# Four of the shift's sixteen conditioning steps moved from slots 49-55 to slots 96-100, the scale's steps one per slot behind them

## The reference

```python
mod = (jax.nn.silu(c) @ w_ada + b_ada)[:, None, :]
sh1, sc1, gt1, sh2, sc2, gt2 = jnp.split(mod, N_MOD, axis=-1)
h = rmsnorm(x, g_pre_mix) * (1.0 + sc1) + sh1
m, ... = token_mixer(h, w_in, ..., w_out, ..., k_past, v_past, s0)
x = x + gt1 * rmsnorm(m, g_post_mix)
h = rmsnorm(x, g_pre_ffn) * (1.0 + sc2) + sh2
f = (silu(h @ w_ffn_gate) * (h @ w_ffn_up)) @ w_ffn_down
x = x + gt2 * rmsnorm(f, g_post_ffn)
```

## Time and profile before

| | us |
|---|---|
| runs | 1507.1, 1503.08, 1507.56; median 1507.1 |
| the profiled execution: its own time | 1503.11 |
| its span, first to last instruction | 1501.4 |
| TensorE busy | 1439.7 (96%) |
| VectorE busy | 913.3 (61%) |
| ScalarE busy | 660.7 (44%) |
| mean granted clock of TensorE | 0.987 |

### The profile page before, as it was taken

One profiled execution on the slowest core, in us unless ns is written; L12 is line 12 of the kernel. 1 busy time (PEld: TensorE's weight loads), 2 busy tenths in 40 slices (PEclk: granted clock), 3 DMA queues, 4 the chain that ended last, 5 costly groups with the idle time before them and its releaser, 6 DMA issues.

```text
span 1501.4 us, 29221 instructions
## 1 busy us (share of the span) xinstructions
PE 1439.7 (96%) x11274; PEld 1274.0 (85%) x11274; DVE 913.3 (61%) x1501; ACT 660.7 (44%) x1277; POOL 105.2 (7%) x205
## 2 busy tenths in 40 slices
PE   7779999998899999998999999999999999999997
PEld 2247787887568787796899999999999999999997
DVE  2243588995687666457657666566665665446444
ACT  1023477776655544336434434444344343334333
POOL 1000311112322200100000000000000000200000
PEclk9979999999899999999999999999999999999999
DMA  9999999999999978996766565665656555855552
GB/s 370 421 362 360 389 387 402 369 333 397 385 373 326 338 259 281 393 328 257 264 184 182 168 193 172 184 179 168 194 177 185 177 171 186 235 182 181 178 179 94
DMA packets 139043, 396.56 MB, mean 264 GB/s; under 512 B 13130, under 2 KB 17393, under 8 KB 126145
## 3 DMA queue, kind: packets, MB, share of 16 engines
q1 hardware_dynamic: 117730, 319.39, 62.9%
q0 software_dynamic: 21232, 76.10, 13.4%
HBM read 382.14 MB, written 11.21 MB: 262 GB/s over the span
## 4 chain that ended last, share of the span: by engine, by line
PE 80%; DMA 12%; DVE 3%; ACT 2%; issue 1%; POOLq 0%; SPq 0%; POOL 0%; DVEq 0%; ACTq 0%
PE ps L1907 23%; PE ps L1908 23%; PE ps L1909 23%; PE ps L1841 4%; DMA ada_s<-in_w_ada 3%; DMA raw<-in_w_in 2%; DMA v_page<-in_cache_v 2%; DMA k_page<-in_cache_k 2%; DMA ada_r<-in_w_ada 2%; PE ps L2039 2%; DMA x_keep<-x_t 1%; PE ps L1965 1%; DVE k_page L1275 1%; DMA k_page<-in_cache_v 1%; PE ps L1884 1%
## 5 line engine op out<-in xcount | busy, mean ns | idle before, releaser
L1907 PE MATMUL ps<-h_hi,w_hi 128*128 128x264 f32 x2304 | 665.7, 289 | 7.6 <-DVE h_lo L1213 3.6
L1908 PE MATMUL ps<-h_lo,w_hi 128*128 128x264 f32 x2304 | 656.5, 285 | 0.0
L1909 PE MATMUL ps<-h_hi,w_lo 128*128 128x264 f32 x2304 | 655.9, 285 | 0.0
L1907 PEld LDWEIGHTS ps<-h_hi,w_hi 128*128 128x128 f32 x2304 | 435.9, 189 | 53.4 <-issue 38.3
L1729 DVE TENSOR_TENSOR w_lo<-raw,w_hi 128x1024 fp32r<-128x1024 f32 x256 | 309.5, 1213 | 275.4 <-ACT w_hi L1018 274.1
L1018 ACT ACTIVATE w_hi<-raw 128x1024 fp32r<-128x1024 f32 x264 | 278.4, 1059 | 405.0 <-PE ps L1909 393.9
L1908 PEld LDWEIGHTS ps<-h_lo,w_hi 128*128 128x128 f32 x2304 | 435.3, 189 | 0.1
L1909 PEld LDWEIGHTS ps<-h_hi,w_lo 128*128 128x128 f32 x2304 | 434.2, 188 | 0.0
L1225 DVE TENSOR_TENSOR w_lo<-raw,w_hi 128x1024 fp32r<-128x1024 f32 x136 | 166.2, 1223 | 162.4 <-ACT w_hi L702 155.1
L702 ACT ACTIVATE w_hi<-raw 128x1024 fp32r<-128x1024 f32 x128 | 134.9, 1055 | 193.4 <-PE ps L1909 162.4
L1908 PE MATMUL ps<-act_lo,w_hi 128*128 (+1 forms) x704 | 200.4, 285 | 0.0
(11 more groups left out here) (336 smaller groups left out, 1211.6 us busy)
## 6 DMA issues: line engine op xcount, KB each, us to landing
ada_r<-in_w_ada SPq DMA_DIRECT2D x64, 1024.0 KB, 9.4
raw<-in_w_in SPq DMA_DIRECT2D x96, 512.0 KB, 8.3
raw<-in_w_ffn_gate SPq DMA_DIRECT2D x88, 512.0 KB, 3.7
raw<-in_w_ffn_up SPq DMA_DIRECT2D x88, 512.0 KB, 3.8
raw<-in_w_ffn_down SPq DMA_DIRECT2D x88, 512.0 KB, 4.1
ada_s<-in_w_ada SPq DMA_DIRECT2D x32, 1024.0 KB, 13.2
k_page<-in_cache_k POOLq DMA_DIRECT2D x64, 512.0 KB, 7.5
v_page<-in_cache_v POOLq DMA_DIRECT2D x38, 512.0 KB, 7.7
```

The lines of the kernel that those rows point to most:

```text
L1907: mm(out, w_hi, xh, start=first, stop=False)
L1908: mm(out, w_hi, xl, start=False, stop=False)
L1909: return mm(out, w_lo, xh, start=False, stop=last)
```

## The change

Part 3 gets 12 steps (n = 16 to 27, slots 25 to 47) and is turned in slot 55 as before. Its last four steps (n = 28 to 31) go to slots 96, 97, 98 and 100, sum up in bank 7 by themselves, are turned in slot 101 and are added on DVE to what `mod_t` holds. Part 4's sixteen steps go to slots 103 to 118, one in each, with the turn in slot 119. The buffers of the steps from slot 96 on are given out anew (five in rotation), and most loads go one SP slot earlier ahead of their step than before. SP's wait ahead of the state loads is for 28 steps instead of 32. On POOL the output of the prompt's V rows goes ahead of that of the samples' K rows. The number of steps, products and bytes loaded is the same; there is one turn more.

```diff
-        ADA_PLACE = [(n + 2) % 4 for n in range(16)] + [n % 2 for n in range(16)] + [2, 3, 4, 2, 3, 4, 5, 6, 3, 4, 5, 6, 4, 5, 6, 4] + \
-                    [(7, 8, 5, 6, 4)[n % 5] for n in range(16)]
+        RING = [(2, k) for k in range(KC)] + [(3, k) for k in range(KC)] + [(4, k) for k in range(KC)] + [(5, k) for k in range(KC)]
+        N3 = KC + 12
+        RING_END = (KC, N3, 2 * KC, 3 * KC, 4 * KC)
+        ADA_PLACE = [(n + 2) % 4 for n in range(16)] + [n % 2 for n in range(12)] + \
+                    [2, 3, 4, 2, 3, 4, 5, 6, 7, 3, 4, 5, 6, 7, 8] + [4 + n % 5 for n in range(21)]
...
-        PARTS = (1, 0, 2, 3, 4, 5)
-        TURN_BANK = (4, 7, 4, 4, 7, 4)
+        PARTS = (1, 0, 2, 3, 3, 4, 5)
+        TURN_BANK = (4, 7, 4, 4, 7, 7, 4)
...
-            (96, 97, 98, 100, 101, 102, 103, 104, 105, 106, 107, 108, 110, 111, 112, 114))})
+            (96, 97, 98, 100, 103, 104, 105, 106, 107, 108, 109, 110, 111, 112, 113, 114, 115, 116, 117, 118))})
...
-        TURN_AT = {20: 2, 55: 3, 115: 4}
+        TURN_AT = {20: 2, 55: 3, 101: 4, 119: 5}
...
+                        if n == N3 + 14:
+
                             sp.wait_ge(rows_out, 64)
...
                 if s == 57:
 
-                    sp.wait_ge(ada_used, 32)
+                    sp.wait_ge(ada_used, N3)
...
-                    act.wait_ge(ada_used, KC * (q - 1))
+                    act.wait_ge(ada_used, RING_END[q - 2])
...
+                if q == 4:
+
+                    mod = MOD[:, KC * p:KC * p + KC, :].rearrange("p (j i) t -> p j i t", j=4)
+                    v.tensor_tensor(mod, src, mod, ALU.add).then_inc(mod_done, 1)
+                    return
```

More of the change, by code:

```diff
@@ L266, in stickbreak_gla_layer @@
         A_SLOT = {n: 3 + 9 * n // 8 for n in range(16)}
-        A_SLOT.update({16 + k: 25 + 2 * k for k in range(16)})
-        A_SLOT.update({32 + k: s for k, s in enumerate(
-            (96, 97, 98, 100, 101, 102, 103, 104, 105, 106, 107, 108, 110, 111, 112, 114))})
-        A_LOAD = {n: A_SLOT[ADA_BEFORE[n]] + 3 for n in range(35, 48) if n not in (38, 39)}
-        A_LOAD.update({32: 94, 33: 95, 34: 98, 38: 101, 39: 102, 48: 113, 49: 116, 50: 118, 51: 120, 52: 121})
+        A_SLOT.update({KC + k: 25 + 2 * k for k in range(N3 - KC)})
+        A_SLOT.update({N3 + i: t for i, t in enumerate(
+            (96, 97, 98, 100, 103, 104, 105, 106, 107, 108, 109, 110, 111, 112, 113, 114, 115, 116, 117, 118))})
+        A_LOAD = {n: A_SLOT[ADA_BEFORE[n]] + 3 for n in range(N3 + 3, 53) if ADA_BEFORE[n] is not None}
+        A_LOAD.update({N3: 94, N3 + 1: 95, N3 + 2: 98, N3 + 6: 102, N3 + 7: 103, N3 + 8: 104, N3 + 14: 111})
         A_AT = {s: n for n, s in A_SLOT.items()}
-        TURN_AT = {20: 2, 55: 3, 115: 4}
+        TURN_AT = {20: 2, 55: 3, 101: 4, 119: 5}
         KP_SLOT = [20 + 2 * n // 3 if n < 18 else 32 + n - 18 if n < 36 else 50 + 2 * (n - 36) // 3 for n in range(TS * PAGES)]
@@ L373, in ada_start, with ring_start @@
                 return ada_v[:, k, PARTS[q] * 2048:PARTS[q] * 2048 + 2048]
+            def ring_start(n):
+                part, k = RING[n]
+                return ada_v[:, k, part * 2048:part * 2048 + 2048]
             for tb in range(TB):
@@ L438, in _ @@
                         ada_load(n)
-                    if 18 <= n < 32 and s == A_SLOT[n - 2] + 3:
+                    if 18 <= n < N3 and s == A_SLOT[n - 2] + 3:
                         ada_load(n)
                     if A_LOAD.get(n) == s:
-                        if n in (32, 33):
-                            sp.wait_ge(av_used, n - 1)
-                        if n == 34:
+                        if n in (N3, N3 + 1):
+                            sp.wait_ge(av_used, n - N3 + 31)
+                        if n == N3 + 2:
                             sp.wait_ge(d_sel, 2)
@@ L641, in _ @@
                                VTOK[:, tb, :]).then_inc(vtok_out, 16)
+            for i in range(2):
+                pool.wait_ge(row_ready, i + 1)
+                pool.dma_start(ks_rows[:, i * 512:i * 512 + 512], KSV[:, i, :]).then_inc(rows_out, 16)
             for i in range(2):
@@ L1084, in _ @@
                     hi_n(W_FFN, p + 1)
-            mod_row(5)
+            mod_row(6)
             for u in range(UPC + 1, UPC + 3):
                 hi_n(W_FFN, u)
-            act.wait_ge(modt, 6)
+            act.wait_ge(modt, 7)
             glu_exp(0)
@@ L1743, in _ @@
                 lo_n(W_FFN, u)
-            mod_part(5)
+            mod_part(6)
             for u in range(UPC + 1, UPC + 3):
@@ L1849, in ada_next @@
             def ada_next(n):
-                if n % KC == 0:
-                    pe.wait_ge(mod_done, 1 if n == 0 else n // KC + 2)
-                    if n == 32:
+                starts = (0,) + RING_END
+                t = max(i for i in range(5) if starts[i] <= n)
+                if n == starts[t]:
+                    pe.wait_ge(mod_done, t + 2 if t else 1)
+                    if n == N3:
                         pe.wait_ge(d_put, 2)
@@ L1857, in ada_next @@
                 pe.wait_ge(ada_in[p], 16 * ADA_COUNT[n])
-                ada_step(AR[p], n % KC, TURN_BANK[n // KC + 2]).then_inc(ada_used, 1)
+                first, last = n == starts[t], n == starts[t + 1] - 1
+                for j in range(4):
+                    ins = mm(ps[32 * j:32 * j + 32, TURN_BANK[t + 2], :], CTK[:, RING[n][1], :], AR[p][:, j * CG:(j + 1) * CG],
+                             start=first, stop=last)
+                ins.then_inc(ada_used, 1)
             def mod_turn(q):
```

23 lines of the change are left out of this document (10 added, 13 removed).

## The result

The changed kernel takes 1508.3 us (median of 20 runs, 1504.4 to 1511.1) against 1504.3 us before (20 runs, 1500.1 to 1508.6): ratio 1.0025, 95% interval 1.0017 to 1.0032, some 3.8 us slower. The forecast was 1505.0 and no change. So the profiles are compared by stages, and what they leave open is measured with edited kernels.

The account below looks back on a forecast made before the run. From 330 us transfers, no longer TensorE's work, were taken to pace the kernel. 5.4 us won and 5.2 given back made 0.2 less: 1505.0 us from the 1505.2 mean of four runs, range 1499 to 1511.

Parts of the forecast that it names:

- Together 5.2 us: Slots 96 to 127: net four added steps, one more turn of four transposes; 5.2 us given back.
- Rival (d): Slots 103 to 118 fall behind DMA, `raw` lands too late for ACT: 1507 to 1514 us; chance 0.05.
- I take 5.4 for the gain at slot 73: the 4.4 of the load and 1.0 of the clock: By slot 73: earlier `raw` load wins 4.4 us, shorter low clock 1.0; bounds nothing to 10.6.
- TensorE could be at slot 56 some 5.5 us sooner: Slots 49 to 55: four removed steps of 1.20 us, 4.8, plus the turn's 0.7 us wait.
- The new wait of 3 us in slot 56: TensorE, arriving earlier, stands about 3 us in slot 56 for DVE's part 3 addition, leaving 2.1 us earlier.
- Those loads and the raw load behind them go out 3.1 us earlier: SP's wait ahead of the state loads is for a step long done, so these loads issue 3.1 us earlier.
- rival (c): SP's earlier issue alone wins 3.1 us, clock drops as before: net 2.1 slower, 1507.3 us; chance 0.2.
- Its 1.05 MB are 2.6 us of transfer that the stretch doesn't have to do: Last removed load, issued at 325.85 us near the full DMA stretch, frees 2.6 us at 396 GB/s.
- Rival (b): No gain at the front, `raw` load and V pages land as before; 5.2 us slower, 1510.4; chance 0.1.
- the `raw` load taking over 29 us: Sign for the rival without any gain: the `raw` load behind the state loads takes over 29 us.
- Rival (a): TensorE keeps its 5.5 us and both clock drops vanish: 10.6 won, net 5.4, 1499.8 us; chance 0.2.
- 1.0 us for a shorter drop at 374 us: Behind 374 us the wait of 3.6 us shrinks to near 1.2, so less low clock: 1.0 us won.

Follow-up runs that it names:

- the kernel with the back alone: Changed kernel with the last four steps of part 3 run again in slots 49, 51, 53 and 55, with their loads: ratio to before 1.0034.
- pairs before: Kernel before with a second step in each of slots 96 and 100 and none in slots 101 and 114: 1502.7 us, ratio 0.9988.
- front only: Changed kernel without the four steps of slots 96, 97, 98 and 100 and their loads: 1510.6 us, ratio to before 1.0039.
- pairs after: Changed kernel with two steps each in slots 96 and 100 and none in 97 and 98: 1506.6 us, ratio to before 1.0012.
- the kernel with late state loads: Changed kernel with the first three state loads issued in slots 60, 62 and 64 instead of 57: 1508.6 us, ratio to before 1.0025.
- the two kernels with the filler: Changed kernel with one step's matmuls more in slot 51, without a load: ratio to before 1.0027; the same with part 3's turn in slot 53: 1.0030.
- the last kernel of the table: Changed kernel with paired steps in slots 96 and 100, turn in slot 53, state loads in slots 60, 62 and 64: 1506.3 us, ratio to before 1.0019.

## Why the prediction was wrong, step by step

**The back: right in its size.** "Together 5.2 us": 5.3 in the profile, 5.2 in the kernel with the back alone. From slot 106 to 118 every slot takes 4.11 to 4.13 us, with no wait for a load, so DMA keeps up; slot 127 to the end is unchanged. Two rows of the last stretch in the changed kernel show the beat:

```profile
638.37 1.06 PE L1879 MATMUL ps<-ada_r,c_t_keep 128*32 128x512 f32 x8
642.48 1.06 PE L1879 MATMUL ps<-ada_r,c_t_keep 128*32 128x512 f32 x8
```

Rival (d) did not happen.

**"I take 5.4 for the gain at slot 73: the 4.4 of the load and 1.0 of the clock": the step that failed.** It was nothing in the profile (counted from slot 48, slot 73 starts 1.3 us later), and 1.4 us by the ratios (1.0034 of the kernel with the back alone less 1.0025; each is uncertain by 1 to 2 us). In slots 48 to 76 the three profiled kernels with the front of before (before, back only, pairs before) take 150.7, 152.0 and 149.4 us, those with the front of after (after, front only, pairs after) 151.9, 151.8 and 148.6: means of 150.7 and 150.8. One profile of this stretch can't tell 1.5 us from none, and the 2.4 us that the first table shows for slots 56 to 76 are no more than this scatter. The term of 4.4 us had the `raw` load land sooner; it landed 1.5 us later. Nor does the stretch hang on it: with the state loads out of its way this load took 8.5 us, and the changed kernel was no faster. The waits from 336 to 450 us did not shrink but grew from 14.5 to 17.6 us; that was one of my signs for being wrong, "if they stay at 14". Why the V pages, 14.8 us of it, come no sooner stays open.

**"TensorE could be at slot 56 some 5.5 us sooner": failed too.** It was 1.1. I had priced four steps by TensorE's own rows, where TensorE had no waits, and took "no wait" to mean that nobody was near. DVE was 0.05 us ahead of TensorE in slot 51. Of the 5.5 us, 1.96 became the wait for the tree. The low clock behind it took some 1.7 (slots 51 and 52 took 7.89 and 3.58 us; in the kernel with late state loads, which waits as long at a clock of 1.00, 6.71 and 3.10). The rest is the sizes: the turn's wait shrank by 0.6 and the four steps gave 1.0 to 1.1 us each, not 1.20. But none of these shares matters by itself: with more work or with a full clock, slot 56 came at 36.0 us just the same, held by ACT's copy, and behind that by ACT's `proj_t`. The most that any edit of this kind got is 1.9 us (35.18 instead of 37.11).

**The new wait of 3 us in slot 56** never came, as TensorE wasn't there early enough to meet it. The mechanism, a wait that takes the place of the one removed, was right; it stood five slots sooner and on another chain.

**"Those loads and the raw load behind them go out 3.1 us earlier": half right.** The state loads did, by 3.0. The `raw` load went out 0.5 us later, counted from slot 48: I had named the split that it needs and not looked up its time, which is only 1.1 us ahead of the old issue, and I hadn't reckoned with an issue of 4 us ahead of it. And the state loads gained nothing: they stood behind a `raw` load whose issue hadn't moved. The Trainium skill's rule that engines take turns between queues ("DMA: Bandwidth & Descriptors", Queues, rings and completion order) led me to rival (c), in which the earlier issue alone was worth 3.1 us. The trace agrees with the rule as far as it shows it, both queues moving side by side (4.43 and 2.19 MB from 330 to 350 us in the changed kernel), and not with what I drew from it: the earlier issue brought nothing, since the load ahead in SP's own queue landed when it did.

**"Its 1.05 MB are 2.6 us of transfer that the stretch doesn't have to do": not so.** The stretch from 330 us was full because of those loads, and with them gone it was not full until 350.

**Which case it was.** Rival (b), "nothing is left of the gain, slower", comes nearest and had one chance in ten: it forecast 5.2 us slower, (c) 2.1, and 3.8 to 4.0 were measured. Its reasons were the full engines and the V pages. The runs add the one that comes first: DVE and ACT set the arrival at slot 56. My test for (b), the `raw` load taking over 29 us, was not met (27.0), so it was the wrong test. That the time stayed inside my range is no merit of the mechanism, as the range took in (b). Rival (a) did not happen.

**The clock.** I counted 1.0 us for a shorter drop at 374 us. That one lasted some 3.4 us instead of 6.9, and the one at 401 us was gone; but there were new ones, of some 3.5 us at 360 us behind a V page's wait of 2.99 us, and in slot 51. The Trainium skill ("TensorE: Matmul & The Clock Gate", Part 1) has the clock fall after idling. The rows agree that drops stand behind waits (1.96 us in slot 51, 1.72 in slot 100 of the kernel with the front alone). They also show waits of 1.95 and 1.96 us behind which the clock stayed, so the length of a wait alone didn't tell me whether a drop would come.

## What to carry to other kernels

A bound engine without waits is no proof that its work there costs its full time: look up when each of its inputs was ready, and count as saved only what lies between that moment and its use. Here a step was free in slots 49, 51, 96 and 100, and cost some 1.2 us in slots 97, 98 and 101 to 118; extra work belongs ahead of a wait on a fixed chain, and two steps there instead of one won 2.4 us in the profile and some 1.8 by the ratio. Look also at what stands ahead of a transfer in its queue: the state loads were issued 3.0 us earlier and landed 0.4 to 1.5 us later, behind a load that had not moved.

## What the runs showed of the hardware

- The same wait of 1.96 us of TensorE, in the same slot, was followed by a low clock in three kernels (0.50 and 0.70 after; 0.57 and 0.58 in the one with the front alone; 0.63 and 0.52 with pairs) and by a clock of 1.00 in the two with late state loads and with the turn in slot 53; in the last kernel of the table, with 1.95 us, it stayed at 1.00 as well. What decides it is not shown. The waits of 0.95 and 0.96 us in the two kernels with the filler brought no drop.
- An issue on SP's queue can itself take long: the row of three state loads has 1.56 us before and 5.10 after, with one of 3.95, and the two `raw` issues behind it 9.57, where one with no queue ahead took 0.37. SP's later issues are held up by this too. It came with three or more loads of the queue under way, though not each time; that the queue has no room then is a guess that no run tests.
- State loads of 0.5 MB landed 6.1 to 7.3 us apart in one queue, 72 to 86 GB/s, while the engines moved 343 to 400 GB/s in all from 340 to 370 us.
